# Expert routing in a two-layer decoder trunk: a gather from rows kept in contraction order, the two experts found by a search for the eight largest, and spare matmuls around the choice

## The reference, cut to what matters

```python
grp_logits = (xt @ w_grp) + b_grp
grp = jnp.argmax(grp_logits, axis=-1)
exp_logits = ((xt @ w_exp) + b_exp).reshape(T, MOE_GROUPS, EXPERTS_PER_GROUP)
in_grp = jnp.take_along_axis(exp_logits, grp[:, None, None], axis=1)[:, 0]
top_v, top_i = lax.top_k(in_grp, TOP_K_INNER)
gate = jax.nn.softmax(top_v, axis=-1) * p_grp[:, None]
...
hid = jax.nn.silu(xk @ w_gate[e]) * (xk @ w_up[e])   # for the rows of expert e
y = hid @ w_down[e]
```

## Time and profile before

| | |
|---|---|
| median of 3 runs | 1435.07 us (1432.77 to 1436.47) |
| time of the profiled execution | 1435.21 us |
| its span | 1433.3 us |
| PE busy, DVE busy, ACT busy | 1115.3, 439.2, 339.7 us |
| mean granted TensorE clock | 0.901 |
| moved by DMA | 489.00 MB, 341 GB/s over the span |

### The profile page before, as it was taken

How to read it: one execution, slowest core, us unless ns; L and a number is a source line. 1 busy time by engine, 2 the same in 40 slices (tenths; PEclk the granted TensorE clock), 3 DMA queues, 4 the chain that set the end, 5 groups by cost and what they waited for, 6 DMA issues and landing times.

```text
span 1433.3 us, 15782 instructions
## 1 busy us (share of the span) xinstructions
PE 1115.3 (78%) x6732; PEld 684.7 (48%) x6732; DVE 439.2 (31%) x855; ACT 339.7 (24%) x561; POOL 65.2 (5%) x120
## 2 busy tenths in 40 slices
PE   6999997857676576776799999997857757566576
PEld 6986786323133232332688877776413323133231
DVE  6744545100101001011766666745100100001001
ACT  4333432101000010001655556542101001010010
POOL 2000000000000000000300006400000000000000
PEclk9999998989788897889999999998979888788898
DMA  9642569999999999999655557678999999999997
GB/s 341 207 170 88 212 257 372 408 428 428 427 427 428 428 428 427 429 427 401 199 183 176 176 176 180 151 298 372 429 429 427 427 428 429 426 429 427 428 428 297
DMA packets 72184, 489.00 MB, mean 341 GB/s; under 512 B 6096, under 2 KB 6304, under 8 KB 47024
## 3 DMA queue, kind: packets, MB, share of 16 engines
q1 hardware_dynamic: 67696, 480.53, 82.5%
q0 software_dynamic: 4000, 7.36, 2.7%
q10 hardware_dynamic: 416, 0.07, 0.0%
HBM read 486.77 MB, written 1.17 MB: 340 GB/s over the span
## 4 chain that ended last, share of the span: by engine, by line
PE 54%; DMA 38%; DVE 3%; ACT 2%; issue 1%; POOL 0%; SPq 0%; DVEq 0%; ACTq 0%
PE triple L1151 10%; DMA ring<-in_exp_up 8%; DMA ring<-in_exp_down 7%; PE triple L358 7%; PE triple L359 7%; PE triple L360 7%; DMA ring_more<-in_exp_gate 6%; DMA ring_more<-in_exp_down 6%; PE bank L1109 4%; PE triple L1173 4%; PE bank L1173 3%; DMA ring_rows<-in_exp_up 2%; DMA ring_more<-in_exp_up 2%; DMA ring<-in_exp_gate 2%; PE bank L358 2%; PE bank L360 2%
## 5 line engine op out<-in xcount | busy, mean ns | idle before, releaser
L1151 PE MATMUL triple<-ring,work 128*32 128x512 f32 x1248 | 262.3, 672 | 102.0 <-DMA ring<-in_exp_up 31.9
L1151 PE MATMUL triple<-ring_more,work 128*32 128x512 f32 x608 | 209.0, 663 | 31.3 <-DMA ring<-in_exp_up 15.2
L1151 PEld LDWEIGHTS triple<-ring,work 128*32 128x32 f32 x1248 | 68.1, 122 | 227.5 <-issue 215.0
L1295 DVE TENSOR_TENSOR work<-work,triple 128x512 f32<-128x512 f32 x16 | 11.0, 688 | 519.3 <-PE triple L1151 519.3
L1109 PEld LDWEIGHTS bank<-work,hn 128*128 128x128 f32 x512 | 124.3, 334 | 40.3 <-issue 36.8
L1109 PE MATMUL bank<-work,hn 128*128 128x128 f32 x512 | 130.1, 410 | 15.4 <-DVE h L1304 12.2
L1173 PE MATMUL triple<-ring,work 128*32 128x512 f32 x288 | 79.0, 779 | 65.5 <-DMA ring<-in_exp_down 25.8
L1304 DVE TENSOR_TENSOR h<-h,bank 128x512 f32<-128x512 f32 x64 | 44.0, 687 | 257.0 <-PE bank L1216 257.0
L1151 PE MATMUL triple<-ring_rows,work 128*32 128x512 f32 x192 | 106.1, 712 | 0.0
L1173 PE MATMUL triple<-ring_more,work 128*32 128x512 f32 x176 | 65.5, 764 | 43.8 <-DMA ring<-in_exp_down 26.2
L340 DVE TENSOR_TENSOR lo_b<-ring,hi_b 128x2048 fp32r<-128x2048 f32 x40 | 90.6, 2289 | 18.7 <-ACT hi_b L333 18.7
(11 more groups left out here) (312 smaller groups left out, 1848.0 us busy)
## 6 DMA issues: line engine op xcount, KB each, us to landing
ring<-in_exp_gate SPq DMA_DIRECT2D x39, 2048.0 KB, 29.3
ring<-in_exp_up SPq DMA_DIRECT2D x39, 2048.0 KB, 29.4
ring<-in_exp_down SPq DMA_DIRECT2D x34, 2048.0 KB, 27.5
ring_more<-in_exp_gate SPq DMA_DIRECT2D x21, 2048.0 KB, 29.0
ring_more<-in_exp_down SPq DMA_DIRECT2D x20, 2048.0 KB, 29.9
ring_more<-in_exp_up SPq DMA_DIRECT2D x17, 2048.0 KB, 29.3
ring<-in_w_kv SPq DMA_DIRECT2D x12, 2048.0 KB, 8.9
ring<-in_ret_w_in SPq DMA_DIRECT2D x11, 2048.0 KB, 9.1
```

The lines of the kernel that those rows point to most:

```text
L1151: last = nc.tensor.matmul(bank[2 + kind][rows, :], m_x[:, k, rows], w[e][:, kk * FF:(kk + 1) * FF], start=(k == 0), stop=(k == KD - 1))
L1295: V.tensor_tensor(m_hid[0:M, :], m_sg[0:M, :], bank[3][0:M, :], ALU.mult).then_inc(s["hid_ready"], 1)
```

## The change

Three things change, in both layers. First, ScalarE writes the normed rows in the order of the contraction: `hn_by_k` lies in the same memory as `hn`, but the 128 values of step k stand side by side. ScalarE now reads `h` at a distance of eight values and writes side by side, and the gather's weights are read side by side instead of at a distance of eight. Second, DVE finds the two experts with one search for the eight largest values and one for their places, for each token tile, and makes the one-hot rows by comparing the places with 0 to 31; the place itself, times 32, is the expert's first slot, so two instructions that computed it fall away for one. Third, `keep_warm(n)` issues n matmuls whose result nobody reads: 6 before the PE's wait for the choice, 4 after the ranks.

```diff
@@ in ffn_norm_act
-                nc.scalar.mul(hn[:, t, :], h[:, t, :], stat[:, 1, t:t + 1]).then_inc(s_hn, 1)
+                nc.scalar.mul(hn_by_k[:, t, :, :], h[:, t, :].rearrange("p (c k) -> p k c", k=KD),
+                              stat[:, 1, t:t + 1]).then_inc(s_hn, 1)
@@
+        def keep_warm(n):
+            for _ in range(n):
+                nc.tensor.matmul(bank[7][:, 0:2 * P], ident, kept[:, 0:2 * P], start=True, stop=True)
@@ in route_pe
+            keep_warm(6)
             pe.wait_ge(s_chosen, layer + 1)
...
             nc.tensor.matmul(bank[5][:, 0:32], ones, A[:, 1, :], start=False, stop=True).then_inc(s["ranked"], 1)
+            keep_warm(4)
@@ in route_dve
             chain(last)
+            best, place_of = tmp(TT, 8), tmp(TT * 8).bitcast(U32).rearrange("p (t i) -> p t i", t=TT)
+            for t in range(TT):
+                last = V.max(best[:, t, :], E1[:, t, :])
+            chain(last)
+            for t in range(TT):
+                last = V.max_index(place_of[:, t, :], best[:, t, :], E1[:, t, :])
+            chain(last)
             hots = tmp(2 * TT, NE)
             hot1, hot2 = hots[:, 0:TT, :], hots[:, TT:2 * TT, :]
-            top1 = first_max(E1, NE, hot1)
-            E2 = tmp(TT, NE)
-            chain(V.scalar_tensor_tensor(out=E2, in0=hot1, scalar=-2.0 * FAR, in1=E1, op0=ALU.mult, op1=ALU.add))
-            top2 = first_max(E2, NE, hot2)
+            for i, hot in enumerate((hot1, hot2)):
+                last = V.tensor_tensor(hot, over_tiles(iota[:, 0:NE], NE), over_last(place_of[:, :, i], NE),
+                                       ALU.is_equal)
+            chain(last)
             V.tensor_tensor(A, hot1, hot2, ALU.add).then_inc(s_chosen, 1)
-            V.tensor_tensor(m_e[:, 8:10], top2, top1, ALU.subtract).then_inc(s_exp_in, 1)
+            V.tensor_tensor(m_e[:, 8:10], best[:, :, 1], best[:, :, 0], ALU.subtract).then_inc(s_exp_in, 1)
...
-            chain(V.tensor_tensor(mine, hots, own.unsqueeze(1).to_broadcast([P, 2 * TT, NE]), ALU.mult))
-            chain(V.tensor_reduce(first4, mine, AX, ALU.add))
+            chain(V.tensor_scalar(first4.rearrange("p (i t) -> p i t", i=2),
+                                  place_of[:, :, 0:2].rearrange("p t i -> p i t"), float(SLOTS), None, ALU.mult))
@@ in gather
-                        last = nc.tensor.matmul(bank[b][:, kk * M:(kk + 1) * M], hn[:, t, 4 * b + kk::KD],
+                        last = nc.tensor.matmul(bank[b][:, kk * M:(kk + 1) * M], hn_by_k[:, t, 4 * b + kk, :],
```

More of the change, by code:

```diff
@@ L28 @@
 I32 = mybir.dt.int32
+U32 = mybir.dt.uint32
 ALU = mybir.AluOpType
@@ L194, in build @@
         hn = place("hn", HN_AT, [P, TT, D])
+        hn_by_k = place("hn_by_k", HN_AT, [P, TT, KD, P])
         xT = place("xT", XT_AT, [P, KD, S])
```

## The result

The change made the kernel faster: 1425.09 us (1423.28 to 1426.74, 6 runs) against 1434.59 (1432.38 to 1437.01), ratio 0.9933 with the interval 0.9918 to 0.9948. Measured a second time, it was 1426.63 (1423.00 to 1431.38, 10 runs) against 1433.47 (29 runs), ratio 0.9955, interval 0.9942 to 0.9969. That is 9.5 us and then 6.8, where 6.3 was forecast. The profiled execution, the fastest of the six, took 1423.28 us, span 1421.5: 11.8 us less than the span before.

A forecast was written before the change was run, and what follows sets the result against it. Weight loads through full DMA engines bound the kernel, except in droughts. Layer 0's 4.0 us, capped at 3.2, plus layer 1's 3.1 (4.0 - 0.9) gave 6.3: 1435.2 - 6.3 = 1428.9 us, range 1425 to 1433.5.

The forecast's parts named there:

- the two droughts: Windows early in each layer where the DMA engines run dry before the refill: 3.2 us lost in layer 0, 4.6 in layer 1.
- ScalarE's hidden cost: ScalarE's read of `h` at a distance of eight: 2.19 us unchanged, up to 5.1, hidden in both cases.
- The choice: DVE's choice of experts after the logits, 2.70 us replaced by 1.46: 1.24 us earlier (0.7 to 1.5).
- the place search: DVE's search for the experts' places, within the choice: no row for it, between 0.43 and 1.2 us, taken as 0.65.
- The gather: First gather's 16 records with weights side by side: 4.22 us to 1.8, 2.4 less at the upper clock, 0.8 at the lower.
- The spare matmuls: Six before the ranks, four behind: clock kept up, ranks 0.4 us shorter; layer 0 on time, layer 1 0.9 us late.
- The caps: An earlier refill is worth at most each layer's drought, 3.2 and 4.6 us, 7.8 together.
- the last group of layer 1: There the PE is the bound; shifting its clock can win or lose 1 to 2 us usually, 4.4 at the extreme.
- The clock low in the gather: Rival: clock drops between spare matmuls and gather; 2.4 us sooner in each layer, 1430.4 to 1432 us; 15%.
- The distance not the price: Rival: the weight read's distance is not what slows the gather; 1.64 us a layer, 3.3 in all, 1431.9 us; 8%.
- Nothing won: Rival: loads issue sooner without gain, because of transfers under way, or the place search costs far more; 1434 to 1436 us; 10%.
- Slower: Rival: spare matmuls at the lower clock push the gather 2.1 us later; 2.6 to 8.6 us lost, 1437.8 to 1443.8; 7%.

## Where the mechanism of the prediction held, and which steps failed

**Right.** The time lay in the two droughts. Predicted 3.2 and 3.1 us for the two layers, 6.3 in all; counted from the logits, 6.5. The 48 us of PE time that the faster gathers gave back (1115.3 to 1067.2 with the order alone) were worth nothing, as said. The price of the distance, ScalarE's hidden cost, and the drop of the gain with a low clock came as described.

**The choice.** Forecast 1.24 us sooner, measured 1.52 (4.41 to 2.89). The term that was too high was the place search, taken as 0.65: two instructions for each tile are there, as the Trainium skill has it (VectorE: DVE Perf Modes, section Two Vector instructions with no wait between them), but they are short, 0.09 and 0.18 us, and the pair ends after 0.43, the lower bound.

**The gather.** Forecast 2.4 us sooner, measured 2.15 (4.22 to 2.07). A record took 0.129, not the 0.110 of the logits.

**The spare matmuls: the step of the sum that failed.** I read the moment of the clock's fall from one execution and carried it over: "in layer 0 the six run from 229.3 almost wholly at the upper clock and end near 232, before the choice", and 0.9 us late in layer 1. It was the other way round. In layer 0 the clock fell at about 225.6, with the PE still busy on the logits (granted 0.75 from 225.50 to 225.75, 0.50 behind it), and was down when they ran, as the windows show:

```profile
225.80:228.00 2.20, 2.20 (x7) 1.75 (x7) 1.83 (x12) 2.18 (x2) 0.00 (x0) 0.50 1.07 447
228.00:229.00 1.00, 1.00 (x4) 0.82 (x3) 0.93 (x9) 1.00 (x1) 0.00 (x0) 0.50 0.84 360
229.00:230.20 1.20, 1.20 (x9) 1.07 (x7) 0.16 (x3) 0.41 (x3) 0.00 (x0) 0.98 1.02 437
```

and the ranks started 4.12 instead of 3.17 us after the logits; in layer 1 they were on time. So the 0.9 us taken off layer 1 should have been nothing there: the refill came 4.11 us sooner, not 3.1. The 0.95 that layer 0 lost were not missed, since the 3.25 us left to its refill are still the whole drought of 3.2. Over the four executions of the changed kernel the ranks were late by 0.95, 0.57, 1.90 and 0.58 us in layer 0 and by 0, 0, 0 and 1.02 in layer 1. In the eight profiled executions that have the search and the six, the ranks were late in layer 0 in five, by 0.57 to 1.90 us, and in layer 1 in two, by 1.02. Either layer can be hit, layer 0 more often; only a spread could have been forecast. The mean lateness, 0.63, is near the 0.45 that the sum held on average, so the sum came out near with its two halves wrong, which is luck.

**The caps.** In the first trace layer 0 gave 3.6 from logits to logits, against a cap of 3.2; over the three executions before and the four of the changed kernel its mean was 2.4 (749.6 to 747.2). Layer 1 gave 4.0 (454.2 to 450.2), against a cap of 4.6 and a forecast of 3.1.

**The range: a term put at nothing.** 1425.09 lies at the very edge of 1425 to 1433.5, 9.5 us below the kernel before and not 6.3. The prediction named the last group of layer 1 as the "one thing" that moves by luck, 1 to 2 us, and gave the stretch ahead of the change no term. That stretch moves by 4.9 us between executions, and in the first pair of traces it fell 3.4 us in the change's favour. With it the 11.8 us between the two spans are 3.4 ahead of the change, 3.25 and 4.11 at the refills, and 0.4 and 0.7 behind them. That the same luck is in the median of the first six runs is likely, but only one of them has a trace; the second measurement, with ten runs, gave 1426.63 and a gain of 6.8.

**The rivals.** The clock low in the gather: true as a mechanism, and held off by the four spare matmuls behind the ranks. The distance not the price: refuted. Nothing won: refuted. Slower: the late spare matmuls cost what they are late, but six are late by 0.6 us on average, not 2.

## What to carry to other kernels

Where a queue of transfers bounds the kernel, look for the windows in which its engines run dry, take their depth as the cap, and count only the work between the last free slot and the next; a page's largest saving of busy time can be worth nothing. Remove the bound that hides another first: here a slow weight read hid the clock, and neither repair was worth its size without the other. Spare matmuls pay only if they end before the engine is needed, so size them by their length at the lower clock; here the four just ahead of the gather mattered most. Before a gain of this size is believed, measure it a second time, and look in both traces at a point ahead of which nothing changed.

## What the runs showed of the hardware

- A float32 weight load read at a distance of one or two values took 192 and 196 ns, at four and eight 329 and 335. For matmul records that is 0.129 us apart side by side, against 0.25 at four and eight.
- ScalarE's read of 1024 float32 values took 1.14 us side by side, 1.22 in pairs and 2.15 at a distance of eight.
- Four small transfers under the weights' stream (162 KB) went with 364 GB/s in place of 424 over 10 us, while the DMA engines showed as busy in both.
- The same code reached the same point between 225.9 and 230.8 us, a spread of 4.9 us over eighteen executions, beside a gain of 6.5.
- The granted clock fell at 225.6 us with the PE busy, and in one execution it showed 1.00 over 5 us in which the matmul records were 0.21 us apart, where 0.12 is the pace of the upper level.
